# Adding the residual rows in the output projection: a vector addition becomes an accumulating transfer of GpSimd's queue, and the turned mix lies 128 bytes further

## What is computed

```python
x = x + gt1 * (jnp.concatenate([att, conv], axis=-1) @ w_out)
h2 = rmsnorm(x, g_n2) * (1 + sc2) + sh2
x = x + gt2 * hierarchical_moe(h2.reshape(B * T, D), ...).reshape(B, T, D)
```

## Time and profile before

| | |
|---|---|
| median of 3 runs | 2188.37 us (2187.49 to 2191.16) |
| profiled execution | 2188.47 us, span 2186.9 us |
| PE busy | 1983.7 us, 91% |
| DVE busy | 1582.0 us, 72% |
| ACT busy | 1050.6 us, 48% |
| POOL busy | 533.8 us, 24% |
| mean granted clock of PE | 0.962 of full speed |
| this stage | from some 940 to 1215 us of the span, after its weights |

### The profile page before, as it was taken

One profiled execution on the slowest core, in us unless ns is written; L12 is line 12 of the kernel. 1 busy time (PEld: TensorE's weight loads), 2 busy tenths in 40 slices (PEclk: granted clock), 3 DMA queues, 4 the chain that ended last, 5 costly groups with the idle time before them and its releaser, 6 DMA issues. The chain is left out here.

```text
span 2186.9 us, 40449 instructions
## 1 busy us (share of the span) xinstructions
PE 1983.7 (91%) x13272; PEld 1590.7 (73%) x13273; DVE 1582.0 (72%) x3149; ACT 1050.6 (48%) x2056; POOL 533.8 (24%) x571
## 2 busy tenths in 40 slices
PE   6999999998999987689999399999899998999976
PEld 3788888886787776378888278788687876778732
DVE  3558888986988888389998568664547674648757
ACT  2312111112888887144453267555436564647623
POOL 1013444430111153015654301001110101010055
PEclk8999999998999999789999599999999999999989
DMA  8686555665667577767777289975758797769978
GB/s 258 236 294 233 210 184 189 228 223 173 201 196 260 183 263 255 251 198 246 257 262 245 81 301 396 347 287 180 253 198 297 278 350 266 259 247 381 398 243 312
DMA packets 221315, 553.21 MB, mean 253 GB/s; under 512 B 28802, under 2 KB 43482, under 8 KB 219929
## 3 DMA queue, kind: packets, MB, share of 16 engines
q1 hardware_dynamic: 170891, 425.60, 55.6%
q0 software_dynamic: 25088, 75.71, 9.7%
q10 hardware_dynamic: 25239, 50.67, 6.7%
HBM read 456.95 MB, written 167.56 MB: 286 GB/s over the span
## 5 line engine op out<-in xcount | busy, mean ns | idle before, releaser
L2530 DVE TENSOR_TENSOR LO<-WIDE,HI 128x2048 fp32r<-128x2048 f32 x128 | 287.1, 2284 | 85.0 <-ACT HI L2452 85.0
L644 DVE SCALAR_TENSOR_TENSOR arena<-arena,tapw 128x512 f32<-128x512 f32 (+3 forms) x435 | 266.4, 691 | 0.0
L2452 ACT CAST HI<-WIDE 128x2048 fp32r<-128x2048 f32 x128 | 238.1, 1909 | 23.1 <-PEq L217 16.2
L2530 DVE TENSOR_TENSOR LO<-W2E,HI 128x2048 fp32r<-128x2048 f32 x64 | 143.8, 2289 | 93.3 <-ACT HI L2452 93.3
L445 POOL TENSOR_TENSOR STATS<-STATS,K 128x1 f32<-128x1 f32 x16 | 134.4, 8400 | 308.1 <-ACT H L497 308.1
L777 PE MATMUL PJ<-WIN_H,HTH 128*128 128x512 f32 x640 | 160.3, 392 | 5.0 <-ACT HTH L505 5.0
L787 PE MATMUL PJ<-WIN_L,HTH 128*128 128x512 f32 x640 | 158.7, 390 | 0.0
L781 PE MATMUL PJ<-WIN_H,HTL 128*128 128x512 f32 x640 | 158.2, 389 | 0.0
L2452 ACT CAST HI<-W2E 128x2048 fp32r<-128x2048 f32 x64 | 118.7, 1904 | 60.5 <-issue 60.5
L777 PEld LDWEIGHTS PJ<-WIN_H,HTH 128*128 128x128 f32 x640 | 118.6, 188 | 32.9 <-issue 9.1
L529 ACT ACTIVATE arena<-PJ 128x512 f32<-128x512 f32 x48 | 28.6, 601 | 231.5 <-PE PJ L787 231.5
(11 more groups left out here) (367 smaller groups left out, 4515.6 us busy)
## 6 DMA issues: line engine op xcount, KB each, us to landing
WIDE<-in_w_expert_gate SPq DMA_DIRECT2D x64, 1024.0 KB, 8.3
WIDE<-in_w_expert_up SPq DMA_DIRECT2D x64, 1024.0 KB
W2E<-in_w_expert_down SPq DMA_DIRECT2D x64, 1024.0 KB
expert_rows<-YE ACTq DMA_DIRECT2D x40, 512.0 KB
expert_rows<-NOROWS POOLq DMA_DIRECT2D x11, 1536.0 KB, 11.7
QN<-q_rows SPq DMA_DIRECT2D x48, 256.0 KB
KN<-out_new_k_prompt SPq DMA_DIRECT2D x48, 256.0 KB, 4.1
VN<-out_new_v_prompt SPq DMA_DIRECT2D x48, 256.0 KB, 3.9
```

The source lines that it names most:

```text
L644: ins = nc.vector.scalar_tensor_tensor(out=out, in0=src, scalar=tap, in1=out, op0=ALU.mult, op1=ALU.add)
L2452: nc.scalar.copy(HI[n][:, cols], raw[n][:, cols]).then_inc(hi_ready[n], 1)
L2530: nc.vector.tensor_tensor(LO[n][:, cols], raw[n][:, cols], HI[n][:, cols], ALU.subtract).then_inc(lo_ready[n], 1)
```

## The change

The addition on DVE, its call, the tile `X3` and SP's loads of x go. GpSimd's round gets `add_rows(i-1)` as its first step: it waits until the gated rows are in `X2`, and issues a transfer that adds the rows of x from memory onto them. `x2_ready` then counts by 16 a tile, when the transfer has landed. Between `MIX` and `MT_H` 128 bytes are left free in each partition; `X3`, which lay ahead of them, held 4096.

```diff
-        NB, ST, CC, X = sb("NB", [P, 3, DATT]), sb("STAT", [P, 3, 2 * HEADS]), sb("CC", [P, KC, P]), sb("X3", [P, D])
+        NB, ST, CC = sb("NB", [P, 3, DATT]), sb("STAT", [P, 3, 2 * HEADS]), sb("CC", [P, KC, P])
...
-        MIX, MTH, MTL = sb("MIX", [P, D]), sb("MT_H", [P, KD, P], F32R), sb("MT_L", [P, KD, P], F32R)
+        MIX = sb("MIX", [P, D])
+        sb("MIX_PAD", [P, P // 4])
+        MTH, MTL = sb("MT_H", [P, KD, P], F32R), sb("MT_L", [P, KD, P], F32R)
...
 # SP, round_
                     if there(i - 1):
-                        sp.wait_ge(x2_ready, i)
+                        sp.wait_ge(x2_ready, i * 16)
                         n = rows_of(i - 1)
                         sp.dma_start(dr["x2"][ds(behind, n)], X2[0:n]).then_inc(x2_out, 16)
-                    if there(i):
-                        n = rows_of(i)
-                        src = t["x_sample"][:, 0] if n == DEC else t["x_prompt"][0, ds(row, P)]
-                        sp.dma_start(X[0:n], src).then_inc(x_in, 16)
...
 # GpSimd
+                def add_rows(i, rows):
+
+                    src = t["x_sample"][:, 0] if rows == DEC else t["x_prompt"][0, ds(i * P if isinstance(i, int) else pool.snap(i * P), P)]
+                    pool.wait_ge(x2_half, i + 1)
+                    pool.sem_inc(placing, 1)
+                    pool.dma_start(X2[0:rows], src, accum_op=ALU.add).then_inc(x2_ready, 16)
+
                 def round_(i):
+                    if there(i - 1):
+                        add_rows(i - 1, rows_of(i - 1))
                     if there(i - 3):
                         keep_weight(i - 3)
...
 # ACT, squares
-                    act.wait_ge(x2_ready, i + 1)
+                    act.wait_ge(x2_ready, i * 16 + 16)
...
 # DVE
-                def added(i, rows):
-                    dve.wait_ge(x2_half, i + 1)
-                    dve.wait_ge(x_in, i * 16 + 16)
-                    nc.vector.tensor_tensor(X2[0:rows], X2[0:rows], X[0:rows], ALU.add).then_inc(x2_ready, 1)
-
...
                     if there(i - 3):
                         weigh(i - 3)
-                    if there(i - 1):
-                        added(i - 1, rows_of(i - 1))
```

More of the change, by code:

```diff
@@ L1663, in output_projection_and_routing @@
         ln_in, bias_in = sem("ln3_in"), sem("router_bias_in")
-        br_in, cc_in, x_in = sem("br_in"), sem("cc_in"), sem("x3_in")
+        br_in, cc_in = sem("br_in"), sem("cc_in")
         astep, exp_b, att_ready, conv_turned, bn_done, ln_rs, y_norm, th_ready = (
@@ L1700, in round_ @@
                 def round_(i):
-                    row, behind, ahead = ((i * P, (i - 1) * P, (i + 2) * P) if isinstance(i, int) else
-                                          (sp.snap(i * P), sp.snap((i - 1) * P), sp.snap((i + 2) * P)))
+                    behind, ahead = ((i - 1) * P, (i + 2) * P) if isinstance(i, int) else (sp.snap((i - 1) * P), sp.snap((i + 2) * P))
                     taken = i + 2 if isinstance(i, int) else sp.snap(i + 2)
```

## The result

| | before | after |
|---|---|---|
| median of four runs, us | 2189.28 | 2272.56 |
| lowest and highest, us | 2187.49 to 2191.16 | 2269.95 to 2275.24 |
| profiled execution, us (span) | 2188.47 (2186.9) | 2269.95 (2268.4) |
| mean granted clock | 0.962 | 0.947 |

The changed kernel takes 1.038 times as long, with a 95% interval of 1.0362 to 1.0398: 83.3 us more between the medians, 81.5 us more between the profiled spans.

The account below looks back on a forecast made before the run. DVE was taken to set the pace, with PE close behind. To 2188.4 us came 66 for eleven adds behind zero rows and 6 for the other adds, making 2260.5, with a range of 2208 to 2310.

Parts of the forecast that it names:

- The chain: From x2 through ACT's squares and rounding copy to DVE's rest and PE's second half: 10.1 us to the next gating.
- The bytes: DMA traffic from the zero rows' issue to the add's landing: 2.88 MB, reached after 9.4 us.
- The landing: The add behind the zero rows lands 10.8 us after their issue, with bounds of 9.4 and 14.2.
- The accumulation: In the add's transfer, the destination is read as well as written: one more pass of 0.52 MB, 10.8 us instead of 9.4.
- the eleven rounds: Tiles 3 to 13, whose adds stand behind zero rows: 21.9 us a round in place of 15.95, 66 us in all.
- Both are of the same queue: On GpSimd's queue the add stands behind the zero rows, issued 0.66 us past the gating's end.
- The rival that the add does not queue behind the zero rows: The add's 6.0 us run from its own issue: x2 at 7.9, rounds of 18.0, 2217 us; chance 17%.
- The rival of a start only after them: Accumulation is dear or starts only when the zero rows have landed: rounds of 28.8 us, 2336 us; chance 13%.
- Rounds without zero rows: Adds of tiles 0, 1, 2 and 14: 1.5 us more each; tiles 15 and 16 hidden; 6 us, ends 3 and 12.
- The clock: PE's clock may drop to 0.50 after standing still, costing PE 3 to 5 us a round; priced 0, up to 10 in all.
- The faster rival: Between gating and squares the add lands early enough, PE becomes the bound, 3 to 6 us won: 2183 us; chance 7%.
- Its condition: For a gain, x2 ready within 5.7 us of the gating's start, 3.8 us from the add's issue at 1.9.

Follow-up runs that it names:

- the plain copy: The changed kernel with a plain transfer in place of the accumulating one, so x overwrites the gated rows: 2182.67 us, ratio 0.9966, total not comparable.
- the first experiment: The changed kernel with GpSimd issuing the zero rows right behind the add of the same round instead of ahead of the next: 2231.49 us, ratio 1.0191.

## Why the prediction was right, and by how much it was off

The forecast was 2260.5 with a range of 2208 to 2310; the median is 2272.56. Slower was right. The loss is 83.3 us where 72.1 were forecast.

- **The chain held.** Squares ahead of the rounding copy on ACT, DVE's rest and PE's second half behind it, GpSimd in step: all as in the rows of a round above. From x2 to the zero rows' issue 11.1 us were forecast; it is 1.69 + 1.60 + 7.57 = 10.86 in the round shown.
- **The bytes held.** 2.88 MB were worked out up to the add's landing, 2.9 MB are measured.
- **The landing was undersized.** 10.8 us after the zero rows' issue were forecast (10.9 by its own rates), 11.56 are measured in the round shown and 11.5 on average. The term that was too small is the bytes' own time, "2.88 MB, reached 9.4 us after": the plain copy, which moves just these, is there after 9.95 us on average (9.4 from its issue in the round shown, and 0.95 ahead of it). The rates of before don't hold to the end; the last 0.2 to 0.3 MB come at 135 GB/s with the copy and at 121 with the add. The accumulation, put at 1.4 us (10.8 less 9.4), was nearly right: it cost 1.6 a round. So the round is 22.43, not 21.9, and the eleven rounds cost 71.3 us, not 66. This is 5 of the missing 11 us.
- **The reason for it was half wrong.** "Both are of the same queue" was a reason that the add lands late. With the zero rows on SP's queue it lands nearly as late (9.9 us against 10.4 after its issue). The rival that the add does not queue behind the zero rows falls, since x2 came at 12.4, not 7.9. The rival of a start only after them (28.8 us a round) falls too: the add lands 2.6 us after them, not 6.0.
- **Rounds without zero rows** cost 7.4 us for a forecast of 6. Tiles 1 and 2 gave 1.2 and 1.4 (forecast 1.5 each); tile 0 gave 3.1, since its add took 7.5 us (5.9 in the first experiment, where nothing was changed for it; what spreads them is open); tile 14 gave 2.0, and tile 15's round was 0.3 shorter.
- **The clock** went as described and didn't cost what it could have. It is 0.50 for 5 us of the round shown; from 1003 to 1250 it is 0.88 on average where it was 1.00, and PE's groups of eight matmuls take 3.78 and 3.05 us instead of 2.0. But DVE's gatings waited for PE only five times at the ends of these eleven rounds, 2.1 us in all. At tile 15 one wait of 2.67 us came.
- **What was left out** is about 1 us ahead of the first gating and 2 at the stage's end, where the last row's chain is open: after the last gating the squares come 6.3 us later, not 2.8. That, the 5.3 us of the landing and the 1.4 of the other rounds are about 10 of the 11.2. The profiled executions are 81.5 us apart and the medians 83.3, which is more than the rest.
- **The faster rival** was well bounded. Nothing to wait for at all gives 3.7 us in the eleven rounds and 5.0 in the stage, inside its 3 to 6. Its condition, a landing within 3.8 us, was far off: even the plain copy with no zero rows ahead took 4.8. The fit of the Trainium skill ("DMA: Bandwidth & Descriptors", "Anatomy of one DMA — SWDGE (gpsimd) path"), 3.2 us for these bytes, is too low here.

## What to carry to other kernels

Before moving work from an engine to a transfer, find out how much the engine's freedom is worth (here 0.3 us a round, since PE is right behind) and how long the result may be late (here 1.8 us), and set against them the whole time from issue to landing. In these runs a transfer that starts only when a result is there had to be priced behind the 1.5 MB issued just ahead of it, on either queue, so move bulk transfers behind it before trusting its time. The last part of it must not be priced at the mean rate (here 121 to 135 GB/s after some 300). A load that is done ahead of time costs only its bytes; the same bytes added on arrival put their full time to landing on the chain.

## What the runs showed of the hardware

- An accumulating transfer of 512 KB into SBUF is issued by GpSimd in 0.96 us, a plain one in 0.59. From issue to landing it took 5.5 us against 4.8 with no bulk transfer ahead, and 10.0 against 8.6 behind 1.5 MB. There it ended in a tail of 2.5 us at 121 GB/s, the plain one in 1.7 us at 135.
- 1.5 MB issued some 0.6 us earlier on SP's queue delay it nearly as much as 1.1 us earlier on GpSimd's own (9.9 us to landing, 10.4). Issued 0.9 to 1.6 us behind it on the other queue they cost it about 1.2 us, and 0.7 us behind it on its own nothing to be seen (6.8 us by the median, 6.7 with none near).
- A GpSimd addition of 128x1024 float32 takes 2.37 us, and while it runs a DVE product of 128x1 with two inputs in SBUF took 2.79 us instead of 0.16. With a scalar operand it took 0.21. A copy of 128x4 float32 took 0.58 instead of 0.17 beside that addition and ended 0.03 us after it, though it has one input only.
